# Latent attention pairs: one order of work per turn on every engine, the sample scores issued among the first pair's projections, and one barrier less at each stage's end

## The reference, cut to what matters

```python
kv = (ckv_all @ P['mla_w_ukv'][l]).reshape(B, S, MLA_HEADS, MLA_NOPE + MLA_V)
k_nope = rms_norm(kv[..., :MLA_NOPE], P['mla_kn_nope'][l])
v = kv[..., MLA_NOPE:]
...
s = jnp.einsum('bqhd,bshd->bhqs', q, k).astype(jnp.float32) * (q.shape[-1] ** -0.5)
p = jax.nn.softmax(jnp.where(mask, s, NEG_BIG), axis=-1)
return jnp.einsum('bhqs,bshd->bqhd', p, v.astype(jnp.float32))
```

## Time and profile before

| | us |
|---|---|
| three runs | 4650.6, 4664.6, 4669.6 (median 4664.6) |
| the profiled execution | 4652.6 |
| its span (first to last instruction) | 4650.8 |
| PE busy in the span | 4282.6 (92%) |
| DVE, ACT, POOL busy | 2276.2, 1644.2, 815.4 |
| latent pairs, layer 1 (922.23 to 1299.57) | 377.3 |
| latent pairs, layer 2 (3243.51 to 3620.47) | 377.0 |

### The profile page before, as it was taken

How to read it: one execution, slowest core, us unless ns; L and a number is a source line. 1 busy time by engine, 2 the same in 40 slices (tenths; PEclk the granted TensorE clock), 3 DMA queues, 4 the chain that set the end, 5 groups by cost and what they waited for, 6 DMA issues and landing times. The chain is left out here.

```text
span 4650.8 us, 74929 instructions
## 1 busy us (share of the span) xinstructions
PE 4282.6 (92%) x29488; PEld 2996.2 (64%) x29488; DVE 2276.2 (49%) x4732; ACT 1644.2 (35%) x3886; POOL 815.4 (18%) x980
## 2 busy tenths in 40 slices
PE   7999998988899989999979999989889999899999
PEld 4666665666656667777446656656666666677774
DVE  3566563355524553534335666633555244535344
ACT  4333433455523342122043334334555243421120
POOL 0011000000010024544300110000000100245443
PEclk9999998999999999999989999989999999999999
DMA  5010012000021122321250100121000211223222
GB/s 202 19 35 15 31 27 83 26 23 16 12 89 56 57 75 88 109 90 68 88 196 22 32 17 29 27 84 35 14 16 11 91 54 57 75 89 109 92 73 81
DMA packets 129151, 280.78 MB, mean 60 GB/s; under 512 B 30041, under 2 KB 55897, under 8 KB 123554
## 3 DMA queue, kind: packets, MB, share of 16 engines
q1 hardware_dynamic: 128802, 275.99, 17.7%
HBM read 230.96 MB, written 42.62 MB: 59 GB/s over the span
## 5 line engine op out<-in xcount | busy, mean ns | idle before, releaser
L1061 PE MATMUL banks<-hT,w_piece 128*128 128x384 f32 x1536 | 537.6, 491 | 0.2
L1061 PEld LDWEIGHTS banks<-hT,w_piece 128*128 128x128 f32 x1536 | 276.8, 191 | 161.4 <-issue 7.1
L2244 PE MATMUL banks<-hT,w_piece 128*128 128x384 f32 x1056 | 354.1, 489 | 1.5 <-ACT sb_gate_raw L2354 1.5
L2244 PEld LDWEIGHTS banks<-hT,w_piece 128*128 128x128 f32 x1056 | 196.1, 190 | 141.4 <-issue 16.7
L2010 DVE SCALAR_TENSOR_TENSOR keysT<-banks,gains,rstd 64x128 f32<-64x128 f32 (+1 forms) x272 | 112.0, 412 | 244.4 <-ACT rstd L1924 241.9
L2651 ACT ACTIVATE gate_kept<-banks 128x288 f32<-128x288 f32 x144 | 59.3, 412 | 433.7 <-PE banks L2563 433.7
L2700 DVE TENSOR_TENSOR gate_quarters<-gate_kept,banks 128x288 f32<-128x288 f32 x144 | 65.4, 454 | 299.3 <-PE banks L2563 294.3
L2700 DVE TENSOR_TENSOR branch_quarters<-branch_kept,banks 128x288 f32<-128x288 f32 x144 | 65.4, 454 | 265.2 <-PE banks L2563 265.1
L2413 DVE TENSOR_TENSOR pass<-pass,constants 128x128 f32<-128x128 f32 x128 | 41.1, 321 | 311.9 <-ACT take L2365 309.3
L2416 DVE TENSOR_TENSOR_SCAN left<-pass,zero 128x384 f32<-128x384 f32 (+7 forms) x144 | 189.8, 1318 | 5.0
L1021 POOL TENSOR_TENSOR state_decayed<-state,decay_of_chunk 128x128 f32<-128x128 f32 x120 | 86.0, 717 | 531.1 <-DVE state L1299 531.1
(11 more groups left out here) (427 smaller groups left out, 9771.2 us busy)
## 6 DMA issues: line engine op xcount, KB each, us to landing
w_piece<-in_w_cols SPq DMA_DIRECT2D x66, 512.0 KB, 4.4
w_ada<-in_w_ada SPq DMA_DIRECT2D x24, 1024.0 KB, 9.5
w_gate_ahead<-in_w_cols SPq DMA_DIRECT2D x48, 512.0 KB, 4.3
w_branch<-in_w_br SPq DMA_DIRECT2D x96, 256.0 KB, 2.9
w_gate<-in_w_cols SPq DMA_DIRECT2D x48, 512.0 KB, 4.3
y_branch<-y_gated SPq DMA_DIRECT2D x12, 1152.0 KB, 8.0
sb_cached_keysT<-in_sbkT SPq DMA_DIRECT2D x8, 1024.0 KB, 7.0
sb_cached_values<-in_sbv SPq DMA_DIRECT2D x8, 1024.0 KB, 5.1
```

Source lines behind the costliest of these rows:

```text
L1061: last = mm(dst, w[0 if kind in ("k", "v") else 1][:, k, :], hT[:, k, c], start=(k == 0), stop=(k == KD - 1))
L2244: last = mm(ps[:, bank[n], 0:TG], w_of[wn][:, k, :], hT[:, k, TG * g:TG * g + TG], start=(k == 0), stop=(k == KD - 1))
```

## The change

At every stage the second barrier is gone; two ranges of 48 semaphore numbers alternate instead. In `latent_pairs` four things change. From the 14th fill of the first pair on (`LA_EARLY = 12`) fills use banks 7, 4, 5, 6 in rotation, so that banks 0 to 3 come free earlier, and the scores of units 0 and 1, their maxima and their exponentials stand among those fills. ACT takes `root` of the fill four earlier ahead of `square` there. Value fills of pairs 1 to 3 use the ring of banks 4 and 5 (with places of their own in it) and no longer banks 6 and 7. And the order in a turn becomes:

- PE: scores of u+2, turns of u, `raw`, value fill, values of u-1, `sums`
- ACT: rows of u-2, `root` of the fill of u-1, columns of u, value copy, `square`, exps of u+2
- DVE: normalise of u, maximum of u+2, `norm` of the fill of u-1

```diff
@@ Stages
-            sems.append(nc.alloc_semaphore(f"{n}_{self.k}", **({} if self.first is None else {"num": self.first + len(sems)})))
...
+                sems.append(nc.alloc_semaphore(f"{n}_{self.k}", num=self.first + self.room * ((self.k + 1) % 2) + len(sems)))
...
         nc.gpsimd.sem_clear(range(lo, hi + 1))
-        nc.all_engine_barrier()
@@ latent_pairs, banks
         if n < START:
-            bank.append((6, 7, 0, 1, 2, 3)[n % 6])
...
+            bank.append((6, 7, 0, 1, 2, 3)[n % 6] if n <= LA_EARLY else (7, 4, 5, 6)[(n - LA_EARLY - 1) % 4])
         else:
-            bank.append(6 + len(norms) % 2)
+            bank.append(6 + len(norms) % 2 if kind == "norm" else None)
...
+        for n in at_step[u]:
+            if fills[n][0] == "value":
+                ring["v", n] = len(ring)
@@ PE
                 if 0 <= n - 3 < START and fills[n - 3][0] == "norm":
                     sums(n - 3)
-            scores(0)
-            scores(1)
+                if n in (LA_EARLY + 5, LA_EARLY + 6):
+                    scores(n - LA_EARLY - 5)
+            for n in range(START):
+                if bank[n] in (4, 5):
+                    released(pe, n)
@@ ACT
             for n in range(START + 4):
+                if 0 <= n - 4 < START and fills[n - 4][0] == "norm":
+                    root(n - 4)
+                if n in (LA_EARLY + 8, LA_EARLY + 10):
+                    exps((n - LA_EARLY - 8) // 2)
                 if n < START:
                     (square if fills[n][0] == "norm" else value_rows)(n)
@@ DVE
+                if n in (LA_EARLY + 3, LA_EARLY + 5):
+                    maximum((n - LA_EARLY - 3) // 2)
```

More of the change, by code:

```diff
@@ L112, in __init__ @@
     def __init__(self, nc):
-        self.nc, self.k, self.first = nc, 0, None
+        self.nc, self.k, self.first, self.room = nc, 0, None, 48
     @contextmanager
@@ L1637, in latent_pairs @@
     uses = [bank[:n].count(bank[n]) for n in range(len(fills))]
+    nth_fill = [sum(b is not None for b in bank[:n + 1]) for n in range(len(fills))]
     find = {(f[0], f[1], f[2]): n for n, f in enumerate(fills)}
@@ L1682, in released, with values_made @@
             eng.wait_ge(free[bank[n]], uses[n] + 1)
+        def values_made(eng, h, group):
+            n = find["value", h, group]
+            if h == 0:
+                released(eng, n)
+            else:
+                eng.wait_ge(ring_free, ring["v", n] + 1)
         def sbank(u):
@@ L1806, in value_rows @@
                 kind, h, (first, count), step = fills[n]
-                begin(n)
+                if h == 0:
+                    begin(n)
+                else:
+                    take_ring(("v", n))
+                b = bank[n] if h == 0 else ring_bank(("v", n))
                 for q in range(count):
                     for k in range(2):
-                        last = mm(ps[:, bank[n], P * q:P * q + P], latT[:, k, P * (first + q):P * (first + q) + P], wkv[h][:, k, P:2 * P],
+                        last = mm(ps[:, b, P * q:P * q + P], latT[:, k, P * (first + q):P * (first + q) + P], wkv[h][:, k, P:2 * P],
                                   start=(k == 0), stop=(k == 1))
-                last.then_inc(fill_ready, 1)
+                last.then_inc(fill_ready if h == 0 else ring_ready, 1)
             def scores(u):
@@ L1975, in _ @@
                 rows(u - 2)
-                for n in mine:
-                    if fills[n][0] == "norm":
-                        square(n)
+                if u >= 1:
+                    for n in at_step[u - 1]:
+                        if fills[n][0] == "norm":
+                            root(n)
                 columns(u)
-                exps(u + 2)
                 for n in mine:
@@ L1985, in _ @@
                     if fills[n][0] == "norm":
-                        root(n)
+                        square(n)
+                exps(u + 2)
         @block.vector
@@ L2034, in _ @@
                     norm(n)
-            maximum(0)
-            maximum(1)
+                if n in (LA_EARLY + 3, LA_EARLY + 5):
+                    maximum((n - LA_EARLY - 3) // 2)
             for u in range(U + 2):
                 normalise(u)
-                for n in at_step.get(u - 1, []):
-                    if u >= 1 and fills[n][0] == "norm":
-                        norm(n)
                 maximum(u + 2)
+                if u >= 1:
+                    for n in at_step[u - 1]:
+                        if fills[n][0] == "norm":
+                            norm(n)
 SB_FILL_STEPS = [u for u in range(2 + 2 * NPT) if u % 3 != 2]
```

45 lines of the change are left out of this document (23 added, 22 removed).

## The result

The changed kernel takes 4672.0 us (median; 4662.6 to 4684.1) where the kernel before takes 4658.0 in the same comparison. The ratio is 1.0028 with an interval of 1.0021 to 1.0036: 13 us slower, 10 to 17. That is inside the 0.5% that I had called no change, and inside the range; but with 17 runs of either kernel it can be told, so the forecast of no change didn't hold.

A forecast was written before the change was run, and what follows sets the result against it. PE was taken as the bound, busy 327.0 of 377.3 us in a stage of latent pairs. Barriers -14.5, start +26 and turns -6 gave +5.5 on 4652.6: 4658 us, no change that can be told, range 4632 to 4682.

The forecast's parts named there:

- The barriers: End of each stage: dropping the second barrier gives back 0.5 us at 29 stages, 14.5 us off.
- The start: First pair's fills and first turns: 4.9 us slower at unchanged clock plus 8 for the clock, 13 per layer, 26 in all.
- fills 1 to 13: Early fills of the start: with root before square PE runs through, 18.2 us against 22.4, 4 off per layer.
- the seven waits: PE's waits in the four-bank round of fills 14 to 24: five of 3.3 us, one 1.0, one 5.0, sum 22.5.
- from the 14th fill to the scores of unit 2: Later part of the start: waits, loads and sample scores make 44.7 us against 33.8 before, 10.9 more.
- the 8 for the clock: In the start, PE's work at the low clock of 0.50 adds 8 us per layer.
- the full 12: In the start, about 12 us more per layer if the clock stays low throughout; by the skill's rule this would be due.
- The first three turns: Turns behind the sample scores: about 14.5 us instead of some 16.5, 2 off per layer.
- The turns: Pairs after the first: new waits 12.9 us against 14, 1 off per pair, three pairs, two layers, 6 off.
- a bound: Turns' term at its limit of 0 off: PE idle for 2.9 us may drop the clock, for about 1.7.
- the clock that stays low through the start and the change of pairs: Rival, slower: full 12 at the start, turns' gain eaten and 7 more, +26, 4679 us; chance 0.23.
- the signs that I had set: Changed profile: pairs' stage 5 to 12 us longer ahead of the first turn, query waits about 3, low clock, late sums.

The follow-up runs named there:

- start_only: The kernel before with only the first pair's fills as changed (banks, early scores of units 0 and 1, root ahead of square): ratio 1.0057, +27 us.
- kept_short: The changed kernel with unread matmuls cut to fit PE's waits in the start and at each change of pairs: ratio 0.9981 to before, -9 us.
- square_first: The changed kernel with ACT's square of a turn ahead of its value copy: ratio 0.9948 to before, -24 us.
- barrier_only: The kernel before with only the second barrier at the end of a stage left out: ratio 0.9972, -13 us.
- root_first: The kernel before with only root ahead of square in the first pair's fills: ratio 0.9955, -21 us.
- pairs_only: The changed kernel with the second barrier put back: ratio 1.0069 to before, +32 us.
- turns_only: The kernel before with only the turns' order and the value fills in the ring changed: ratio 1.0008, +4 us.
- six_banks: The changed kernel with six banks in the start and the scores of units 0 and 1 behind the last fill: ratio 0.9954 to before, -21 us.
- kept_busy: The changed kernel with unread matmuls, seven ahead of each of five late raws and eleven ahead of the first turn: ratio 1.0086 to before, +40 us.
- norm_first: The changed kernel with DVE's norm ahead of its maximum in a pair's last turn: ratio 0.9983 to before, -8 us.
- best_of_parts: The changed kernel with the edits of six_banks, square_first and norm_first together: 4561.6 us, ratio 0.9809 to before.
- best_kept: best_of_parts with six unread matmuls in PE's 5.0 us wait ahead of the first sample scores: 4558.2 us, ratio 0.9784 to before.

## Why the prediction was wrong

**The barriers** were sized right: -14.5 forecast, -13 measured alone (-9 by the two profiles' other stages, 0.3 us each).

**The start** came out right as a sum, 13 forecast per layer and 13.9 in the trace up to the end of the third turn (72.7 to 86.6); start_only measured 27 for the 26. Its parts: fills 1 to 13 took 18.1 us for 18.2; the seven waits were those listed; from the 14th fill to the scores of unit 2 it took 52.3, where 44.7 and the 8 for the clock make 52.7. The first three turns took 16.3 and not 14.5. By kept_short the clock's part is 7.5 in layer 2 and at least 5.9 in layer 1, for the 8 that I took. So a clock that was taken a little too dear and turns that were taken too cheap cancelled in part: that the sum is so near is some luck.

The rule of the Trainium skill that I set beside it ("TensorE: Matmul & The Clock Gate", section "HAM oscillation — how this bites in real kernels") is about bursts that are shorter than the waits between them; by it I called the full 12 due. The trace doesn't bear the full 12 out, as the clock came back between the waits (mean granted clock 0.72 and 0.71). Its section "A second HAM failure mode: psum-queue depth-cycling", which I said tells the same, tells of a clock that goes to and fro between the two levels, and that is nearer to what the rows show:

```profile
936.59:961.00 24.41, 17.70 (x111) 13.44 (x109) 6.19 (x17) 6.80 (x17) 2.23 (x16) 0.72 0.00 1
961.00:988.88 27.88, 14.27 (x64) 11.76 (x64) 10.60 (x32) 8.04 (x21) 0.00 (x0) 0.71 0.00 1
```

**The turns** are the step that failed: -6 forecast, +4 measured alone (0 to 8). I counted the waits rightly: 7.2 per pair behind value copies (square_first gave back 7.5), 2.9 at a change of pairs (2.91), 0.7 in steps 13 and 15 (0.66). With the clock held, in kept_short, pair 1 is 0.3 shorter than before's at the same clock of 1.00, of the order of the 1 us that I had. What I had named as a bound and not taken, that PE idle for 2.9 us drops the clock "for about 1.7", happened at every change of pairs in both layers; and at the third the clock stayed low not for 3.4 but for 10.2 us, so that the last stretch lost 5.3. Probably that is because hardly any fills are left there and small waits follow; no run tests that, and in three of the twelve layers named below it was 3.4 or 6.8 us. Per layer the changed kernel loses 1.7 + 1.7 + 5.3 = 8.7.

Not all of the 8.7 belonged in the sum, since the kernel before pays a part of it too. Its trace held the evidence., which I read as the step from pair 0 to pair 1, is the step to pair 2; before's waits at its three changes were 1.54, 1.89 and 2.25, and behind the third, which none of my rows showed, the clock fell. Weight loads at that change, and the clock behind:

```profile
1242.27 0.14 PEld L1854 LDWEIGHTS banks<-constants,exponentials 128*128 128x128 f32 x1
1244.66 0.30 PEld L1842 LDWEIGHTS banks<-keysT,queriesT 96*128 96x128 f32 x2 [2.25 <-issue]
```

```profile
1244.93:1248.33 3.40, 3.40 (x6) 1.26 (x6) 1.28 (x4) 0.67 (x2) 0.00 (x0) 0.50 0.00 0
```

The last stretch tells how much. In the eight profiled layers with before's turns (before, barrier_only, start_only, root_first) it took 54.8 to 60.6 us, 57.8 in the mean, where 54.8 is the time at a clock of 1.00: 3.0 lost. In the twelve with the new turns and the 2.9 us wait (changed, pairs_only, turns_only, six_banks, square_first, kept_busy) it took 59.5 to 62.4, 61.6 in the mean, where kept_short's 57.1 is the time at 1.00: 4.5 lost. My estimate from these rows: the change added 1.7 + 1.7 + 4.5 - 3.0 = 4.9 per layer, 10 in both. That turns the forecast of -6 into the +4 measured, and the sum of +5.5 into +16, inside the 10 to 17.

One of the rivals, the clock that stays low through the start and the change of pairs, had this mechanism for the turns (7 more), but put it together with a full 12 at the start, which didn't come. Of the signs that I had set, the stage came out 17.8 us longer and not 5 to 12, 12.9 of it ahead of the first turn; the waits for DVE's queries, the low clock there and the sums behind value copies came as described.

## To carry to other kernels

Price a wait of PE with the low clock that may follow it: a wait of 2.9 us cost 1.7 us more at the first two changes of pairs and 2.4 to 5.3 at the third, so one long wait for several short ones can be a loss at an equal sum. Look for the same loss in the kernel before, at every place and not at one, since only the difference counts. Where a handover between engines has spare order, put the step that the next engine waits for first (root ahead of square, square ahead of copy, norm ahead of maximum: 89 us together with the barriers and the turns' order, without one instruction less on PE). And before a round gets fewer banks to let other work in early, check that something independent still stands between a fill's sums and the raw that needs its bank.

## What the chip showed that I had not expected

Work added to PE made the kernel faster: 26 matmuls per layer that nobody reads, and three more at each change of pairs, took 22 us off the changed kernel, by the clock alone, as the waits stayed as long as they were.

The same 403 matmuls of the last stretch, in the order of before, took 54.7, 57.3 or 60.7 us in different layers and kernels, in step with the granted clock. Two layers of one execution of barrier_only, the wait at the third change and the stretch:

```profile
1240.25 0.41 PEld L1844 LDWEIGHTS banks<-keysT,queriesT 96*128 96x128 f32 x2 [2.24 <-issue]
...
3555.41 0.30 PEld L1844 LDWEIGHTS banks<-keysT,queriesT 96*128 96x128 f32 x2 [2.24 <-issue]
```

```profile
1233.85:1294.50 60.65, 50.86 (x403) 32.98 (x402) 33.76 (x100) 30.81 (x80) 4.53 (x10) 0.89 0.03 11
3549.02:3603.76 54.74, 45.06 (x403) 30.10 (x402) 33.75 (x100) 30.65 (x80) 4.53 (x10) 1.00 0.04 12
```

So one profiled execution has some 6 us per layer of luck in this place, and the 27 us between the two profiles are to be read beside the 13 of the timed runs. The wait in front is 2.23 to 2.25 us in all eight layers with before's turns; in two of them the clock held behind it, in three it stayed low for 3.4 us and in three for 10.2. Why one layer gets the one and another the other stays open. With norm_first the stretch took 55.4 or 55.5 in all six layers that have its edit (its own two, best_of_parts' and best_kept's): behind the shorter wait, 1.3 us, the clock held each time.
